# Another order inside the SSD groups of a hybrid SSD and MLA layer

## The reference

```python
proj = x @ w_in                     # gates | z | xBC | dt | q_a | kv_a
g_ssm, g_mla = split(sigmoid(gate_pre + b_gate))
# SSD branch: 8 groups of 4 heads
xbc = silu(conv4(xbc));  y = ssd_scan(xh, dt, a, B, C) + D * xh
yg = rmsnorm_by_group(y * silu(z)) * ssm_norm_g
y_ssm = yg @ w_ssm_proj
# MLA branch
y_mla = attention(...) @ w_mla_proj
mix = (g_ssm * y_ssm + g_mla * y_mla) @ w_out
h = LN1(ALPHA * x + mix);  y = LN2(ALPHA * h + relu(h @ w_up)**2 @ w_down)
```

## Time and profile before

| what | value |
|---|---|
| median of 3 runs | 823.72 us (823.61 to 824.08) |
| the profiled execution's own time | 823.72 us |
| its span, from the first to the last instruction | 821.8 us |
| granted TensorE clock, mean | 0.995 |
| busy: PE, DVE, ACT, POOL | 800.4, 590.9, 478.9, 86.2 us |

### The profile page before, as it was taken

The page is one execution under the profiler, slowest core; times in us unless marked ns, Lnnn a source line. Parts: engine busy times, 40 slices in busy tenths (PEclk is TensorE's granted clock), DMA queues, the critical chain, the costliest instruction groups (busy, mean ns, idle before and its releaser), DMA issues.

```text
span 821.8 us, 15721 instructions
## 1 busy us (share of the span) xinstructions
PE 800.4 (97%) x6359; PEld 768.0 (93%) x6359; DVE 590.9 (72%) x980; ACT 478.9 (58%) x833; POOL 86.2 (10%) x174
## 2 busy tenths in 40 slices
PE   8999999999999999899999999999999999999994
PEld 7998999999899898799999999999999999999993
DVE  5996946836746759798888988675688887655554
ACT  5883854845755668644566545434457887633432
POOL 0223112111111002000000000000000000001212
PEclk9999999999999999999999999999999999999998
DMA  8557445335335234343444444655545555555531
GB/s 302 167 172 270 129 130 154 107 130 169 109 106 178 78 106 143 103 141 123 129 148 139 137 136 128 224 159 173 156 154 159 175 155 166 168 158 175 157 127 59
DMA packets 34809, 123.33 MB, mean 150 GB/s; under 512 B 4272, under 2 KB 4928, under 8 KB 34480
## 3 DMA queue, kind: packets, MB, share of 16 engines
q1 hardware_dynamic: 30960, 109.49, 42.8%
q0 software_dynamic: 3008, 10.98, 3.9%
q10 hardware_dynamic: 768, 1.84, 0.6%
HBM read 118.26 MB, written 4.04 MB: 149 GB/s over the span
## 4 chain that ended last, share of the span: by engine, by line
PE 70%; DVE 15%; ACT 9%; issue 3%; DMA 2%; ACTq 0%; DVEq 0%
PE ps_acc L436 12%; PE ps_acc L437 11%; PE ps_acc L438 11%; DVE wlo L1325 4%; PE ps_row L437 3%; PE ps_row L438 3%; PE ps_row L436 3%; ACT whi L936 2%; PE ps_cb L437 2%; PE ps_tr L437 2%; PE ps_tr L438 2%; PE ps_cb L438 2%; PE ps_tr L436 2%; PE ps_cb L436 2%; DVE seg L1610 2%
## 5 line engine op out<-in xcount | busy, mean ns | idle before, releaser
L1325 DVE TENSOR_TENSOR wlo<-wraw,whi 128x1024 fp32r<-128x1024 f32 x203 | 247.2, 1220 | 162.6 <-ACT whi L936 161.8
L936 ACT CAST whi<-wraw 128x1024 fp32r<-128x1024 f32 x203 | 212.3, 1046 | 126.3 <-DMA wraw<-in_wst 126.0
L436 PE MATMUL ps_acc<-xh,whi 128*128 128x288 f32 x560 | 170.9, 305 | 1.7 <-DVE mixm L1670 1.1
L437 PE MATMUL ps_acc<-xl,whi 128*128 128x288 f32 x560 | 165.2, 295 | 0.0
L438 PE MATMUL ps_acc<-xh,wlo 128*128 128x288 f32 x560 | 165.0, 295 | 0.0
L436 PEld LDWEIGHTS ps_acc<-xh,whi 128*128 128x128 f32 x560 | 105.3, 188 | 9.8 <-issue 7.2
L437 PEld LDWEIGHTS ps_acc<-xl,whi 128*128 128x128 f32 x560 | 105.4, 188 | 0.5
L438 PEld LDWEIGHTS ps_acc<-xh,wlo 128*128 128x128 f32 x560 | 105.3, 188 | 0.0
L1382 DVE SCALAR_TENSOR_TENSOR cv<-xp,vec,cv 128x292 f32<-128x292 f32 x96 | 50.2, 522 | 7.9 <-ACT cv L998 5.5
L436 PE MATMUL ps_acc<-o_h,whi 128*128 128x288 f32 x128 | 39.5, 308 | 0.0
L437 PE MATMUL ps_acc<-o_l,whi 128*128 128x288 f32 x128 | 37.8, 295 | 0.0
(11 more groups left out here) (461 smaller groups left out, 2305.4 us busy)
## 6 DMA issues: line engine op xcount, KB each, us to landing
wraw<-in_wst SPq DMA_DIRECT2D x203, 512.0 KB, 3.6
side<-in_ukT POOLq DMA_DIRECT2D x8, 256.0 KB, 4.0
side_v<-in_ukT POOLq DMA_DIRECT2D x8, 256.0 KB, 3.7
out_ssm<-s_out POOLq DMA_DIRECT2D x8, 256.0 KB, 2.5
x<-in_xT ACTq DMA_DIRECT2D x4, 288.0 KB, 4.7
ax<-in_xT POOLq DMA_DIRECT2D x1, 1152.0 KB, 6.1
out_y<-d SPq DMA_DIRECT2D x4, 288.0 KB, 2.1
ckvT<-in_cacheT POOLq DMA_DIRECT2D x1, 1024.0 KB, 7.2
```

The lines of the kernel that those rows point to most:

```text
L436: pe.matmul(out, w, mh, start=first, stop=False)
L437: pe.matmul(out, w, ml, start=False, stop=False)
L936: act.copy(whi[:, s % RING, :], wraw[:, s % RING, :]).then_inc(split_hi, 1)
L1325: tt(wlo[:, s % RING, :], wraw[:, s % RING, :], whi[:, s % RING, :].bitcast(F32), ALU.subtract).then_inc(split_lo, 1)
```

## The change

The two gate chunks gs and gm come before the two z chunks in every group, in the list of chunks and in the queues of PE, ACT and DVE. On PE the sum of squares of group 0 moves behind `cb_products(1)`, and the chunk drawn forward into group 0's end is gs of group 1. On ACT the root of the group before moves from the group's start behind its second `z_block`, followed by a new Exp of one column into `spare`, which makes the Exp table the loaded one; `sample_decays(g + 1)` comes right after `squares(g)`. On DVE `decay_log(1)` goes ahead of `end_state(0)`, and `o_low(2)` and `o_low(3)` into groups 0 and 1 behind `start_state`. The norm steps `normed`, `norm_high` and `norm_low` run three groups behind, `inverse_root` two; those of the last groups run after the loop.

```diff
--- before.py
+++ after.py
@@ -104,7 +104,7 @@
         names += [("qb", i, 2), ("qb", i, 0), ("qb", i, 1), ("k", i, 0), ("k", i, 1), *x[0:5]]
         names += [("v", i, 0), ("v", i, 1), *x[5:7]]
     for g in range(GROUPS):
-        names += [("z", 2 * g), ("z", 2 * g + 1), ("gs", g), ("gm", g)]
+        names += [("gs", g), ("gm", g), ("z", 2 * g), ("z", 2 * g + 1)]
         if g:
             names += [("m", g - 1, 0), ("m", g - 1, 1)]
     names += [("m", GROUPS - 1, 0), ("m", GROUPS - 1, 1)]
@@ -277,6 +277,7 @@
         rstd = after("rstd", [P, 2, T])
         tm = after("tm", [P, 2, T])
         mixt = after("mixt", [P, 2, T])
+        spare = after("spare", [P, 1])
 
 
         mix_h = at("mix_h", [P, KB, T], Z_XH, F32R)
@@ -812,15 +813,17 @@
             decay_rows(0)
             for g in range(GROUPS):
                 if g != 1:
-                    dense(("z", 2 * g), open_turn(("z", 2 * g)))
+                    dense(("gs", g), open_turn(("gs", g)))
                 pe.wait_ge(silu_done, XB + GROUPS + g + 1)
                 tokens(g, 0)
                 cb_products(g)
+                if g == 1:
+                    square_sums(0)
+                dense(("gm", g), open_turn(("gm", g)))
+                tokens(g, 1)
+                dense(("z", 2 * g), open_turn(("z", 2 * g)))
+                tokens(g, 2)
                 dense(("z", 2 * g + 1), open_turn(("z", 2 * g + 1)))
-                tokens(g, 1)
-                dense(("gs", g), open_turn(("gs", g)))
-                tokens(g, 2)
-                dense(("gm", g), open_turn(("gm", g)))
                 outputs(g)
                 states(g)
                 if g:
@@ -834,8 +837,7 @@
                     dense(("m", g - 1, 1), out, o_rows, 8, False, True)
                     square_sums(g)
                 else:
-                    dense(("z", 2), open_turn(("z", 2)))
-                    square_sums(0)
+                    dense(("gs", 1), open_turn(("gs", 1)))
             out = open_turn(("m", GROUPS - 1, 0))
             dense(("m", GROUPS - 1, 0), out, o_rows, 0, True, False)
             dense(("m", GROUPS - 1, 1), out, o_rows, 8, False, True)
@@ -1157,6 +1159,10 @@
                 act.activation(e_row[:], ps_tr[:, 384:512].rearrange("p (h i) -> p h i", h=HPG),
                                ACT.Exp).then_inc(erow_done, 1)
 
+            def exp_table():
+
+                act.activation(spare[:], v1(V_EPS), ACT.Exp)
+
             def z_block(g, k):
                 key = ("z", 2 * g + k)
                 wait_used(act, key)
@@ -1190,30 +1196,32 @@
             act.wait_ge(setup_done, 1)
             sample_decays(0)
             for g in range(GROUPS):
+                ahead(("gs", g))
+                decays(g)
+                if g == 0:
+                    conv_out_block(CB - 1)
+                gate(("gs", g), tz[:, g, :], g)
+                ahead(("gm", g))
+                gate(("gm", g), tm[:, g % 2, :], KB + g)
+                if g >= 3:
+                    norm_high(g - 3)
                 ahead(("z", 2 * g))
-                decays(g)
+                z_block(g, 0)
+                if g == 0:
+                    o_high(3)
+                ahead(("z", 2 * g + 1))
+                z_block(g, 1)
                 if g:
                     root(g - 1)
-                if g == 0:
-                    conv_out_block(CB - 1)
-                z_block(g, 0)
-                ahead(("z", 2 * g + 1))
-                z_block(g, 1)
-                ahead(("gs", g))
-                gate(("gs", g), tz[:, g, :], g)
-                if g == 0:
-                    o_high(3)
-                ahead(("gm", g))
-                gate(("gm", g), tm[:, g % 2, :], KB + g)
+                if g + 1 < GROUPS:
+                    exp_table()
                 if g:
                     ahead(("m", g - 1, 0))
                 squares(g)
-                if g:
-                    norm_high(g - 1)
+                if g + 1 < GROUPS:
+                    sample_decays(g + 1)
                 if g:
                     ahead(("m", g - 1, 1))
-                if g + 1 < GROUPS:
-                    sample_decays(g + 1)
 
 
             def mix_high(b):
@@ -1222,7 +1230,9 @@
 
             ahead(("m", GROUPS - 1, 0))
             root(GROUPS - 1)
+            norm_high(GROUPS - 3)
             ahead(("m", GROUPS - 1, 1))
+            norm_high(GROUPS - 2)
             ahead(("s", 0, 0))
             norm_high(GROUPS - 1)
             ahead(("s", 1, 0))
@@ -1674,45 +1684,50 @@
             decay_log(0)
             conv(CB - 1)
             for g in range(GROUPS):
-                ahead(("z", 2 * g))
+                ahead(("gs", g))
                 if g >= 2:
                     mla_gated(g - 2)
                 tokens(g, 0)
                 ending(g, 0)
-                if g == 0:
-                    o_low(2)
-                ahead(("z", 2 * g + 1))
+                if g >= 3:
+                    normed(g - 3)
+                ahead(("gm", g))
                 products(g)
                 tokens(g, 1)
                 ending(g, 1)
-                ahead(("gs", g))
+                ahead(("z", 2 * g))
                 tokens(g, 2)
                 ending(g, 2)
                 start_state(g)
-                if g == 1:
-                    o_low(3)
-                if g:
-                    inverse_root(g - 1)
-                ahead(("gm", g))
+                if g < 2:
+                    o_low(2 + g)
+                if g >= 3:
+                    norm_low(g - 3)
+                if g >= 2:
+                    inverse_root(g - 2)
+                ahead(("z", 2 * g + 1))
                 gated(g)
+                if g == 0:
+                    decay_log(1)
                 end_state(g)
                 square_add(g)
                 if g:
                     ahead(("m", g - 1, 0))
-                if g:
-                    normed(g - 1)
-                if g + 1 < GROUPS:
+                if 0 < g < GROUPS - 1:
                     decay_log(g + 1)
                 if g:
                     ahead(("m", g - 1, 1))
-                if g:
-                    norm_low(g - 1)
 
 
             ahead(("m", GROUPS - 1, 0))
             mla_gated(GROUPS - 2)
+            normed(GROUPS - 3)
+            ahead(("m", GROUPS - 1, 1))
+            inverse_root(GROUPS - 2)
+            norm_low(GROUPS - 3)
+            normed(GROUPS - 2)
             inverse_root(GROUPS - 1)
-            ahead(("m", GROUPS - 1, 1))
+            norm_low(GROUPS - 2)
             normed(GROUPS - 1)
             ahead(("s", 0, 0))
             norm_low(GROUPS - 1)
```

## The result

The changed kernel takes 817.26 us in the median of 4 runs (816.90 to 818.36), the kernel before 823.90 beside it. The ratio is 0.9921, with a 95% interval of 0.9909 to 0.9933: 6.6 us faster. The profiled execution took 817.52, its span is 815.6 us against 821.8.

The account below looks back on a forecast made before the run. TensorE bounds the kernel, so only its waits count: 0.27 + (1.48 - 0.27) - 0.77 + 2.72 + 1.29 + 0.36 + 1.40 = 6.5, taken as 6.4, from 823.72 to 817.3 us; range 816.5 to 819.4.

Parts of the forecast that it names:

- The bound: Whole stage: TensorE works in 97% of the span, so only its waits, 6.3 us in groups 0 to 2, matter.
- Group 0 and the step to group 1: Group 1's transposes start at 337.02 instead of 338.50: gain 1.48 us, of which 0.27 is the moved sum.
- The `btok` wait: Group 0: block 1's copy comes 0.27 us earlier, and a wait of nearly 1.5 us stays.
- The moved sum of squares: Group 0's sum behind group 1's products: finds VectorE late and gives back 0.27 + 0.5 = 0.77 us.
- Group 1: Root and loads behind the last z chunk: the 1.71 and 0.59 us waits go, gain 2.72 us by starts.
- Group 2 and the steady groups: Norms three groups behind: gains 1.29 and 0.36 us in group 2, 0.28 in each of groups 3 to 7.
- Tanh: ScalarE's tanh after Exp needs no table load, price 0; with a load of 1.28 us, 0.3 in group 1.
- The tail: After group 7: two more norms on VectorE ahead of the split for s(3,0); cost 0, slack 0.7 us.
- Rival (c): It ends slower, as a long ScalarE block before the squares delays VectorE's queue; begins 3.7 us longer; chance 0.03.
- holes: Room in VectorE's queue: 1.4 us at the copy, 1.1 before block 0, 0.3 before `decay_log`, 2.8 in all.
- the MLA bank: Steady groups: the bank of gm is wanted 4.5 us after the gs chunk's start and free at 2.8.
- the later `o_low(2)`: Group 0: VectorE does it later, so its split starts at 321.93 instead of 322.19; gain 0.27 us.

Follow-up runs that it names:

- the seven experiments named above: Seven follow-up runs that leave the stretch from decay rows to group 0's first transposes as the changed kernel has it; it takes 4.26 to 4.30 us there.
- e4: Changed kernel with group 0's end as before: state and sum of squares ahead of `decay_log(1)`, sum on TensorE ahead of group 1; 817.02 us.
- e10: Changed kernel with the root at the group's start, no one-column Exp, and a third `rstd` buffer; 819.39 us.
- e3: Changed kernel with the z chunks ahead of the gate chunks again; 817.07 us.
- e6a: Changed kernel with one more pair of one-column Sqrt and Exp ahead of the squares, 3.0 us more ScalarE work; 824.53 us.
- e6b: Changed kernel with two more pairs of one-column Sqrt and Exp ahead of the squares, 6.0 us more ScalarE work; 846.45 us.
- e8: Kernel before with only the norms moved three groups behind, two `rstd` buffers; 837.92 us.
- e2: Changed kernel with the root back at the group's start and without the one-column Exp; 837.08 us.
- e1: Changed kernel with the norm steps one group behind again; 827.67 us.
- e11: Changed kernel with products and sum of squares reordered in groups 0 and 1, z chunks first, no one-column Exp; 815.59 us.

## Why the prediction was right, and where it was not

The forecast was 817.3. By its steps:

- **The bound.** The waits of TensorE were the whole gain: the stage lost 6.44 us, forecast 6.3 to 6.5, and nothing came from elsewhere.
- **Group 0 and the step to group 1.** From the first decay rows to group 1's first transposes it took 26.06 us before and 24.90 after, 1.16 less; I had 1.48. Two things were off: the first transposes waited 0.14 longer (0.52 instead of 0.38), which the seven experiments named above do not show; and for the hand-off from the decay subtraction to TensorE I took 0.06 us, while both traces show 0.25 (before 338.24 to 338.50, after 337.49 to 337.74). The `btok` wait stayed, with 1.33 us.
- **The moved sum of squares.** Its wait was 0.26 us, not 0.5: it starts at 339.12, and was ready at 338.86. But the sum itself, with the restart of the chunk behind it, took 0.48 instead of the 0.27 that I took. From the first transposes of group 1 to block 1's it is 4.41 us before and 5.15 after: 0.74, where I had 0.77, by two errors that cancel. With the gain ahead of it this part as a whole is worth 0.28 us (e4), where I had 0.44; the hand-off accounts for the difference.
- **Group 1.** Its cycle lost 2.03 us; 2.72 - 0.77 = 1.95 forecast. From block 1's transposes to block 2's it is 6.22 us before and 3.50 after, the 2.72 exactly. e10 puts the root's share of the stage at 2.5 us.
- **Group 2 and the steady groups.** 1.71 us in group 2, forecast 1.65; 0.30 in each of groups 3 to 6 and 0.34 behind group 7's first transposes, forecast 0.28.
- **Tanh.** No load before a tanh, and 23 loads in the stage, as forecast. The Trainium skill ("ScalarE: Activation LUTs", table sets) puts exp and tanh into one set, and the trace agrees: the tanh at 339.67 follows the exponentials without a load. The other figure of that page (section "What ACT_TABLE_LOAD costs"), a drain that makes a switch 2.66 us, is not seen: root and both loads stand within 0.02 us of each other. One reading was wrong: the second load of the earlier trace rows is for Silu after the root, not after Exp. Silu after Exp has its load too, in group 0 of the trace before at 318.81. The price that I gave a load ahead of the second cast, 0.3 us in group 1, is what e3 shows.
- **The tail.** The split for s(3,0) started at 526.21 and took 1.22, TensorE starts that chunk at 528.12. I had 0.7 us of slack; it is 0.7:

```profile
525.34 0.95 DVE L1668 SCALAR_TENSOR_TENSOR yt<-xc,vec,rstd 128x288 f32<-128x288 f32 x2
526.21 1.22 DVE L1335 TENSOR_TENSOR wlo<-wraw,whi 128x1024 fp32r<-128x1024 f32 x1
```

- **Rival (c), mis-sized.** I added holes to 2.8 us and let them all be used up before TensorE waits. But the steps listed another deadline in the same cycle, the MLA bank, wanted at 4.5 and free at 2.8. That slack, 1.7 us, comes first; e6a and e6b measure 1.75. In the changed kernel's group 3 the bank is free at 388.82 and its chunk starts at 390.35, 1.53 us of slack, and a hole of 0.20 before `decay_log` lies ahead of it: 1.73. The kernel was nearer to that cliff than the text said. As six groups pay and not seven, "slower" would have begun at 1.75 + 6.4/6 = 2.8 us of extra work, an estimate, and not at 3.7; e6a with its 3.0 is 1 us slower than the kernel before.
- **What I missed** is the wait on the `rstd` buffer. It changed nothing in the forecast, as the change moves norms and root together; that the steps did not need it is luck. Late norms with the early root (e8, e2) are 14 us slower than the kernel before, and the late root with norms one group behind (e1) is 4 us slower, by the MLA bank. The gains of the parts were therefore not additive, which the text never considered.

Open: the later `o_low(2)` is credited with 0.27 us in group 0, and the wait there did fall from 1.60 to 1.33, but no run undoes it alone. The 0.3 us of the chunk order rest on starts in single traces (e3, e11), as the times cannot tell so little.

## What to carry to other kernels

When a loop is bound by one engine with a few short waits, list every deadline of the cycle with its slack; the smallest on the delayed queue is the room that there is, and holes further down it don't help. Before a step is moved by whole iterations, look at how many buffers its operand has, and which engine waits for the release: here the late norms and the late root gain together, and with the two buffers either without the other made the kernel slower than before. Undo the parts one at a time afterwards: here the new chunk order, after which the change is named, gave 0.3 us of the 6.6. And compare starts group by group, as a short wait is in no list and small differences in other groups can hide it in the sum.

## What the runs showed of the hardware

A table load does not always wait with the activation that needs it. In `z_block` it ran at 344.54, while the SiLU behind it still waited 0.77 us for TensorE, so that all of its 1.28 us lay under the wait. The load ahead of the root in e8 did stand behind the wait for `yt` (3.06 us of idle time before the load at 423.01). And the stage ran at granted clock 1.00 before and after, although its busy share in a cycle rose from 25.57 of 25.66 us to all of 25.35.
